# A two-layer diffusion transformer block with 64 expert passes: expert 0's down product moved into the second gather, and VectorE's overflow list cut in two

## The reference, cut to what matters

```python
experts, gates = route(h_flat, router_w, router_b)   # top 2 of 32 experts for each token, softmax gates
# tokens are sorted by expert; each block xb of one expert e:
(jax.nn.silu(xb @ w_gate[e]) * (xb @ w_up[e])) @ w_down[e]   # 1024 -> 512 -> 1024
# times the gate, summed back into the tokens:  x = x + g2 * out
```

## Time and profile before

| | |
|---|---|
| median of 3 runs | 1360.57 us (1358.97 to 1361.22) |
| profiled execution | 1365.24 us, span 1363.4 us |
| TensorE busy | 1243.5 us (91%), 5042 matmul records |
| VectorE, ScalarE, GpSimd busy | 410.0, 208.4, 69.9 us |
| bytes read from HBM | 485.04 MB, mean 357 GB/s |
| granted TensorE clock | mean 0.97 of full speed |

### The profile page before, as it was taken

The page is one execution under the profiler, slowest core; times in us unless marked ns, Lnnn a source line. Parts: engine busy times, 40 slices in busy tenths (PEclk is TensorE's granted clock), DMA queues, the critical chain, the costliest instruction groups (busy, mean ns, idle before and its releaser), DMA issues.

```text
span 1363.4 us, 13716 instructions
## 1 busy us (share of the span) xinstructions
PE 1243.5 (91%) x5042; PEld 517.2 (38%) x5046; DVE 410.0 (30%) x861; ACT 208.4 (15%) x437; POOL 69.9 (5%) x86
## 2 busy tenths in 40 slices
PE   6999988889999999899988899899999998988986
PEld 3445544545333333233332366453333333322322
DVE  4286646566211111111111145541111121111112
ACT  2212116611110111010111111121111110110100
POOL 0122000000000000000000000000000000000000
PEclk8999989998999999999999999899999999989989
DMA  9958677274899999999999994649999999999993
GB/s 355 379 202 339 233 272 302 101 294 166 333 422 421 422 422 422 422 423 421 422 423 422 417 408 187 260 179 405 422 422 421 422 421 422 423 421 423 422 423 161
DMA packets 81216, 486.54 MB, mean 357 GB/s; under 512 B 6176, under 2 KB 7712, under 8 KB 32032
## 3 DMA queue, kind: packets, MB, share of 16 engines
q1 hardware_dynamic: 79168, 481.91, 86.6%
q10 hardware_dynamic: 2016, 4.21, 0.9%
HBM read 485.04 MB, written 1.05 MB: 357 GB/s over the span
## 4 chain that ended last, share of the span: by engine, by line
PE 60%; SPq 18%; DMA 12%; DVE 6%; ACT 2%; issue 2%; another core or an unknown queue 0%; POOL 0%; DVEq 0%; ACTq 0%
PE PS L761 20%; SPq L300 14%; PE PS L780 10%; DMA ring<-in_moe_w_up 10%; PE PS L598 8%; PE PS L788 5%; SPq L305 4%; PE PS L568 2%; PE PS L661 2%; PE PS L882 2%; PE PS L900 2%; PE PS L753 2%; DMA ring<-in_attn_w_in 2%; PE PS L625 1%; DVE stat L1347 1%
## 5 line engine op out<-in xcount | busy, mean ns | idle before, releaser
L761 PE MATMUL PS<-ring,KQH 128*64 128x512 f32 x2048 | 480.5, 613 | 32.4 <-DMA ring<-in_moe_w_up 30.9
L761 PEld LDWEIGHTS PS<-ring,KQH 128*64 128x64 f32 x2048 | 146.2, 141 | 313.4 <-issue 277.4
L780 PE MATMUL PS<-ring,KQH 128*64 128x512 f32 x1024 | 230.8, 592 | 0.9 <-ACT KQH L1083 0.9
L1589 DVE COPY TMP<-PS 64x512 f32<-64x512 f32 x64 | 43.7, 683 | 460.9 <-PE PS L780 460.9
L780 PEld LDWEIGHTS PS<-ring,KQH 128*64 128x64 f32 x1024 | 73.1, 137 | 146.6 <-issue 145.2
L788 PE MATMUL PS<-TMP,KQH 128*128 128x512 f32 x256 | 118.4, 605 | 1.6 <-DVE TMP L1589 1.6
L598 PE MATMUL PS<-ring,KQH 128*128 128x512 f32 x256 | 116.6, 599 | 0.0
L1066 ACT COPY TMP<-PS 64x512 f32<-64x512 f32 x64 | 37.2, 581 | 455.9 <-PE PS L780 455.9
L1604 DVE TENSOR_TENSOR KQH<-KQH,PS 128x256 f32<-128x256 f32 x64 | 38.7, 605 | 203.1 <-ACT KQH L1091 203.1
L435 POOL COPY KQH<-KQH 128x512 f32 x62 | 38.1, 614 | 859.2 <-PE PS L761 766.5
L788 PEld LDWEIGHTS PS<-TMP,KQH 128*128 128x128 f32 x256 | 46.0, 189 | 73.6 <-issue 70.3
(11 more groups left out here) (233 smaller groups left out, 810.3 us busy)
## 6 DMA issues: line engine op xcount, KB each, us to landing
ring<-in_moe_w_gate SPq DMA_DIRECT2D x128, 1024.0 KB, 26.6
ring<-in_moe_w_up SPq DMA_DIRECT2D x128, 1024.0 KB, 26.6
ring<-in_moe_w_down SPq DMA_DIRECT2D x64, 2048.0 KB, 27.6
ring<-in_ada_w SPq DMA_DIRECT2D x23, 2048.0 KB, 16.0
ring<-in_attn_w_in SPq DMA_DIRECT2D x2, 4096.0 KB, 12.8
ring<-in_attn_w_in SPq DMA_DIRECT2D x2, 2048.0 KB, 21.3
ring<-in_attn_w_out SPq DMA_DIRECT2D x1, 4096.0 KB, 13.9
ring<-in_pool_w_in SPq DMA_DIRECT2D x1, 4096.0 KB, 27.9
```

Of the source, the lines that this page charges most:

```text
L761: ins = mm(PS[64 * f:64 * f + 64, 4, :], xs[:, k, 0:SLOTS], gu_w[s][:, :, k, 256 * f:256 * f + 256], start=k == 0, stop=k == KC - 1)
L780: ins = mm(PS[64 * f:64 * f + 64, 6, :], lhs, dn_w[s][:, c, 512 * f:512 * f + 512], start=c == 0, stop=c == 3)
L1589: return V.tensor_copy(y_sb[64 * second:64 * second + 64, 0:512], PS[0:64, 6, :])
```

## The change

Both layers run the same code, so each edit acts twice. TensorE: the transposes come after chunk 1 of the second gather instead of chunk 2, and the down product of expert 0 comes after chunk 2 instead of after chunk 7. VectorE: `overflow_tiles` keeps its first four instructions and moves ahead of `spread_v(L, 1, 0)`; the other eight are a function `overflow_slots` at the old place. One more instruction waits for its predecessor (`reduce_sum` into `tile_e` is now linked). No instruction is added or removed.

```diff
                     if k >= 2:
                         pe.wait_ge((L.xs_v, L.xs_a)[k % 2], 4 + k // 2)
                     gather(1, k).then_inc(L.xg_done, 1)
-                    if k == 2:
+                    if k == 1:
                         pe.wait_ge(L.h_ready, 1)
                         pe.wait_ge(L.sg_ready, 1)
                         transposes(sg).then_inc(L.tr_done, 1)
-                pe.wait_ge(L.t_ready, 1)
-                pe.wait_ge(L.dn_in[L.slot(0)], 16)
-                down(L.slot(0)).then_inc(L.dn_done, 1)
+                    if k == 2:
+                        pe.wait_ge(L.t_ready, 1)
+                        pe.wait_ge(L.dn_in[L.slot(0)], 16)
+                        down(L.slot(0)).then_inc(L.dn_done, 1)
                 pe.wait_ge(L.gu_in[L.slot(1)], 32)
                 pe.wait_ge(L.xw_ready, 1)
...
                 link(V.tensor_tensor(cmp, cum.unsqueeze(1).broadcast_to(wide), tiles(C_IOTA), ALU.is_le))
-                V.reduce_sum(tile_e[:, 0:OVER], cmp, AX)
+                link(V.reduce_sum(tile_e[:, 0:OVER], cmp, AX))
+
+            def overflow_slots(L):
+
...
                 link(V.tensor_tensor(cmp2, cmp2, cmp, ALU.subtract))
...
+                overflow_tiles(L)
                 spread_v(L, 1, 0)
                 hidden(1)
                 spread_v(L, 1, 2)
-                overflow_tiles(L)
+                overflow_slots(L)
                 spread_v(L, 1, 4)
                 spread_v(L, 1, 6)
```

More of the change, by code:

```diff
@@ L1557, in overflow_tiles @@
                 link(V.tensor_tensor(cmp, cum.unsqueeze(1).broadcast_to(wide), tiles(C_IOTA), ALU.is_le))
-                V.reduce_sum(tile_e[:, 0:OVER], cmp, AX)
+                link(V.reduce_sum(tile_e[:, 0:OVER], cmp, AX))
+            def overflow_slots(L):
+                ov, cum, before, tile_e = rt(5, 32), rt(11, 64)[:, 32:64], rt(12, 32), rt(7, 8)
+                cmp = rt(0, 7 * 32).rearrange("p (i e) -> p i e", i=OVER)
+                cmp2 = rt(8, 7 * 32).rearrange("p (i e) -> p i e", i=OVER)
+                tile_s = rt(7, 24)[:, 8:16]
+                wide = [P, OVER, NE]
                 link(V.tensor_tensor(cmp2, cmp2, cmp, ALU.subtract))
```

## The result

The changed kernel took 1367.11 us (median of 5 runs, 1365.62 to 1370.89), the kernel before 1360.7 us on the same occasion (5 runs, 1358.97 to 1363.89). The ratio is 1.0044, 95% interval 1.0026 to 1.0061: slower by some 6 us, where 2.1 us were forecast and the range ended at 1365.8. In two later comparisons the same kernel stood at 1.0019 (1.0005 to 1.0033) and 1.0023 (1.0004 to 1.0042). Over all 30 runs of it the mean lies 3.6 us above the mean of before, with two standard errors of 1.0 us. So the sign and the place were right, the size was 1.2 to 3 times the forecast, 1.7 times by the mean of all runs.

What follows compares the result with a forecast made beforehand. Bound by the DMA weight stream (421 to 423 GB/s). Stream starts later by 1.0 to 1.3 us (layer 0) and 0.8 to 1.08 (layer 1), taken as 2.1, on median 1360.57 gave 1362.7 us; range 1359.8 to 1365.8.

Steps and rivals of the forecast that it cites:

- what decides: Expert start: expert 1's down product, through expert 4's down rows, decides stream's start; layer 0 1.0 to 1.3 us later.
- the steps that cost nothing: Second gather: list's first four instructions (1.45 us) fit VectorE idle time, other eight hide under down product, 1.39 us stall goes.
- the new wait: Before expert 1's gate/up product: TensorE waits for GpSimd's window, starting 1.3 us later in layer 0, 1.08 in layer 1.
- the fall: TensorE's clock halves in the 2.3 us pause before expert 1: 1.7 to 2.9 us a layer slower; chance 0.16.
- Window not waited for: GpSimd's window is ready when chunk 7 ends: expert 1 starts 0.95 us earlier, 1358.7 us in all; chance 0.11.
- Swallowed: Expert 1's delay finds slack before expert 4's down rows, so the stream starts as before: 1360.6 us; chance 0.13.
- The contention of GpSimd's copy with VectorE: GpSimd's window copy beside VectorE's `lower_outputs` copy could lengthen, adding part of 0.61 us; left out of the sum.

Runs made afterwards that it cites:

- list last: Kernel before, with VectorE's whole overflow list moved behind its last read-out of the second gather, TensorE's order unchanged: ratio 0.9984, run again 0.9988.
- split only: Kernel before, with only VectorE's part of the change (overflow list split), TensorE's order unchanged: ratio 0.9985.
- no window: Changed kernel, with the first half of expert 1's gate/up product reading expert 0's dense columns instead of waiting for GpSimd's window: ratio 0.9988.
- one or two matmuls in the pause: Changed kernel plus constant matmuls ahead of TensorE's wait for GpSimd's window: ratio 1.0007 with one, 1.0009 with two.
- four matmuls: Changed kernel plus four constant matmuls (3.43 us) ahead of TensorE's wait for GpSimd's window: ratio 1.0040.

## Why the prediction was right in kind and wrong in size

**Right: what decides.** Expert 4's down rows, not expert 3's, open the unbroken stream. Their issue moved by -1.6 (list last), -1.2 (split only), -0.7 (no window), +1.4 to +3.4 (the new order, with and without one or two matmuls in the pause) and +2.7 us (four matmuls), and the stream by +1.3 to +1.6, +0.9 to +1.1, +0.7 to +1.0, -0.8 to -3.8 and -1.9 to -2.5. The lead of 2.7 us at 16 us turned into a lag, as forecast, in every kernel with the early down product and a wait for the window.

**Right: the steps that cost nothing.** The list's first half fits into VectorE's idle time, the other half lies under the down product, and the stall goes. The two halves tried alone bear it out: VectorE's gives 1.2 us a layer, TensorE's takes back more than that.

**Right in kind, short by 0.4 us a layer: the new wait.** The term was 1.3 and 1.08 us, measured are 1.70 and 1.47. The GpSimd lag was as assumed (348.16 - 347.11 = 1.05). The 0.4 us lie in seams that I had set at nothing or too low: 0.07 ahead of the down product, 0.10 behind it, 0.14 in chunks 3 to 7 (4.70 us for 4.56) and 0.09 between GpSimd's copy and TensorE. The wait itself, 2.3 us forecast, was 2.40 and 2.18. In the stream the pure delay is 2.1 to 2.6 us over both layers (the four profiles in which the clock stayed up), so the term of 2.1 us was nearly right.

**The step that failed: no term for the clock in the sum.** The forecast let the clock stay at 1.00. I had priced the fall, at 1.7 to 2.9 us a layer, but as a rival with a chance of 0.16. I argued that 2.3 us are less than 1.12 + 1.84 and that the stall of 1.39 us had done nothing. The runs showed a fall in 6 of 10 passes behind pauses of 2.18 and 2.40 us, at 1.5 to 1.7 us each. That is 1.9 us on average over both layers, nearly as much as the whole forecast: 1362.7 becomes 1364.6.

The reading behind it was at fault. I had set 1.56 us, with 3.65 us for the next 16 matmuls, against 1.84 us with 5.35, as if a bound lay between the earlier trace rows. The same trace has a wait of 1.54 us, behind the same 1.12 us for `h_sb`, where the clock fell:

```profile
631.85 5.35 PE L761 MATMUL PS<-ring,KQH 128*64 128x512 f32 x16 [1.54 <-DMA ring<-in_moe_w_up]
```

And in the kernel with only the list split it fell behind 1.12 + 0.61 us, a shorter standstill than the 2.3 us in question (granted clock 0.50 from 1106 to 1108 us):

```profile
1103.82 0.44 PE L771 MATMUL PS<-const,KQH 128*128 128x128 f32 x2 [1.12 <-DVE KQH L1612]
1104.87 5.35 PE L761 MATMUL PS<-ring,KQH 128*64 128x512 f32 x16 [0.61 <-DMA ring<-in_moe_w_up]
```

So the comparison with 2.96 us could not carry a forecast of no fall, and these rows give no bound. At this place of the layer, pauses of 0.4 to 1.45 us left the clock up in 6 of 6 passes. The Trainium skill (TensorE: Matmul & The Clock Gate, Part 1), whose sentence that activity releases the throttle I had set against the change, names no length in it, but had the kind right; I gave the row of the 1.39 us stall too much weight.

**The rest of the 6 us.** Two lags of the stream and 6 falls in 10 account for some 2.3 + 1.9 = 4.2 us, inside 3.6 +- 1.0 of all runs and inside the first comparison's interval (3.5 to 8.3 us). Over the five profiles with the pause, the two stages up to the last combine are 901.1 us long on average, 3.5 more than in the one profile of before. The first five runs of the changed kernel lay higher (mean 1367.8, the 24 runs of the two later comparisons 1365.6). Some 2 us of the 6 in the first comparison stay unexplained: whether they are spread between executions or something of that occasion, no run here shows.

**The other rivals.** "Window not waited for" gave the right answer to its own condition: with the wait taken out, the kernel is at 0.9988, 1.6 us below before (0 to 3.3), for the 1.9 worked out. It just isn't this kernel. "Swallowed" was wrong: of the lag of 5.4 us in the kernel with four matmuls, 4.4 us were in the stream and 3.4 to 7.5 us at the end.

The contention of GpSimd's copy with VectorE, for which I had named the Trainium skill (GPSIMD Engine Reference, section 1), did not lengthen the copy. Two windows took 1.30 us, from 348.16, beside VectorE's L1598 (347.94 to 348.61), the same as before. L1598 reads from PSUM, so that this is no test of two SBUF inputs; in the list-last kernel the copies ran beside such an instruction (L1562) and took 1.31 us.

## What to carry to other kernels

When a block of work is moved, ask what waited behind its cover: the stall that one sees goes, and the wait that the block hid comes out. An earlier DMA issue is worth only what the next issue in the same queue lets through; sum the bytes against time in both profiles, and see whether the lead survives. A pause that two small ones are merged into can cost more than both, through TensorE's clock: fill it or keep it short, and price the fall as a term of the sum, with its chance, wherever the trace shows even one fall behind a standstill of that length or a shorter one.

## What the runs showed of the hardware

The fall of the clock behind a pause of one length is not certain: the same 2.40 us in layer 0 brought it down in 4 of 5 profiles, 2.18 us in layer 1 in 2 of 5. Late in a layer it falls behind waits for DMA in every profile, and there too one length can go either way: with 1.54 us the next 16 matmuls took 5.35 us, with 1.56 us 3.65, in one trace. This may be one source of the spread between executions, which no run here tested: in layer 1 of the kernel before, the last wait (2.83 us) was followed by a half product of 6.54 us, and the layer's last combine stood 449.92 us behind the second gather's first matmul, against 447.70 in layer 0, where the last wait was 0.31 us.

Beside GpSimd's copies one small instruction of VectorE was held up. In the list-last kernel two copies ran from 343.77 to 345.08, and the cast of the overflow list (L1564), 0.17 us long in the kernel before, took 0.47 us and ended at 345.10:

```profile
344.63 0.47 DVE L1564 CAST KQH<-TMP 128x7 int32<-128x7 f32 x1
```

In layer 1 it was the instruction before it (L1563), 0.48 us from 910.49, and the copies ended at 910.94. Both profiles of this kernel show the same two, each ending within 0.03 us of the second copy; the other instructions of the list that ran beside the copies kept their length within 0.02 us. What the held one waits for, no run here shows.
